# Sixteen partitions of a sample on each eighth partition, and the far zone of the caches copied in five-row packets, in a two-layer decoder trunk

## What is computed

```
h = rms_norm(x); a_val, a_glu, a_gate, b_val, b_gate, q, k, v, c_gate = split(h @ w_in)      # 1024 -> 3200
ya = silu(layer_norm(causal_conv31([state_conv, a_val * sigmoid(a_glu)]))) * silu(a_gate)
yb = pooled(b_val, windows 2/4/8/16) @ pool_w * scale * silu(b_gate)
q, k = rope(rms_norm(q)), rope(rms_norm(k))
kk, vv = [cache_k, k], [cache_v, v]
o = softmax attention over offsets 0..128, 0,4..512 and 0,16..2048 (three dilations, 129 keys each)
yc = o * silu(c_gate)
x = x + [ya, yb, yc] @ w_out
new_k, new_v = last 2048 rows of kk, vv        # per sample: the cache moved up by one row, and the new row
```

## Time and profile before

| what | us |
|---|---|
| median of three runs | 413.34 (411.63 to 413.67) |
| the profiled execution, on the device | 411.31 |
| its span, first to last instruction | 409.5 |
| PE, PEld busy | 347.4, 268.5 |
| DVE, ACT, POOL busy | 231.8, 99.2, 56.7 |
| moved by the DMA engines | 158.20 MB, mean 386 GB/s |

### The profile page before, as it was taken

One profiled execution on the slowest core, in us unless ns is written; L12 is line 12 of the kernel. 1 busy time (PEld: TensorE's weight loads), 2 busy tenths in 40 slices (PEclk: granted clock), 3 DMA queues, 4 the chain that ended last, 5 costly groups with the idle time before them and its releaser, 6 DMA issues.

```text
span 409.5 us, 4582 instructions
## 1 busy us (share of the span) xinstructions
PE 347.4 (85%) x1534; PEld 268.5 (66%) x1534; DVE 231.8 (57%) x518; ACT 99.2 (24%) x234; POOL 56.7 (14%) x100
## 2 busy tenths in 40 slices
PE   3899999977899699899799999974899699899500
PEld 2688888855677355788588888852677455688300
DVE  1526998898769734301326998898769654310100
ACT  3301144312533323011200135321623314001100
POOL 3702020202111112202022010202012022000000
PEclk9999999976899999999899999998899899999955
DMA  8999999999999999999999999999999999999993
GB/s 291 413 413 338 416 415 412 409 341 415 410 398 416 406 357 389 407 417 418 409 408 366 388 416 417 419 390 407 403 387 381 411 359 376 420 378 362 362 368 143
DMA packets 49033, 158.20 MB, mean 386 GB/s; under 512 B 5400, under 2 KB 19938, under 8 KB 47986
## 3 DMA queue, kind: packets, MB, share of 16 engines
q0 software_dynamic: 19968, 84.94, 53.4%
q1 hardware_dynamic: 19276, 38.16, 25.3%
q10 hardware_dynamic: 9766, 34.82, 21.5%
HBM read 139.35 MB, written 104.42 MB: 595 GB/s over the span
## 4 chain that ended last, share of the span: by engine, by line
PE 66%; DVE 20%; ACT 4%; issue 3%; DMA 1%; ACTq 0%; SPq 0%; DVEq 0%
PE pj L585 34%; PE pj L722 14%; PE psc L656 7%; DVE yc L1140 4%; DVE tok L1080 3%; DVE ssc L1083 3%; PE ptr L508 3%; DMA vt<-in_x_sample 1%; DVE spsum L1109 1%; PE ps L700 1%; PE psc L624 1%; PE ps L542 1%; PE psc L623 1%; ACT sc L882 1%; DVE sc L1045 1%
## 5 line engine op out<-in xcount | busy, mean ns | idle before, releaser
L585 PE MATMUL pj<-hT,wt 128*128 128x264 f32 x800 | 194.0, 401 | 3.4 <-DVE hT L995 3.4
L585 PEld LDWEIGHTS pj<-hT,wt 128*128 128x128 f32 x800 | 156.5, 199 | 34.8 <-issue 7.7
L1140 DVE SCALAR_TENSOR_TENSOR yc<-u_ext,cst,yc 128x256 f32<-128x256 f32 x180 | 76.2, 480 | 2.8 <-DVE u_smp L1023 0.6
L722 PE MATMUL pj<-mix,wt 128*128 128x264 f32 x256 | 59.5, 387 | 0.0
L722 PEld LDWEIGHTS pj<-mix,wt 128*128 128x128 f32 x256 | 48.0, 190 | 8.0
L503 POOL DMA_DIRECT2D out<-in_cache_v_win x48 | 28.2, 594 | 166.3 <-issue 166.3
L503 POOL DMA_DIRECT2D out<-in_cache_k_win x48 | 28.3, 596 | 136.9 <-issue 130.2
L1210 DVE TENSOR_TENSOR xT<-xT,pj 128x264 f32<-128x264 f32 x16 | 6.9, 430 | 53.2 <-PE pj L722 53.2
L656 PE MATMUL psc<-vt,spm 128*48 128x384 f32 x80 | 27.5, 495 | 0.0
L821 ACT ACTIVATE ex<-pj 128x264 f32<-128x264 f32 x22 | 8.6, 390 | 76.9 <-PE pj L585 62.7
L656 PEld LDWEIGHTS psc<-vt,spm 128*48 128x48 f32 x80 | 9.7, 126 | 14.9 <-issue 14.8
(11 more groups left out here) (165 smaller groups left out, 318.0 us busy)
## 6 DMA issues: line engine op xcount, KB each, us to landing
out<-in_cache_k_win POOLq DMA_DIRECT2D x32, 1080.0 KB, 76.7
out<-in_cache_v_win POOLq DMA_DIRECT2D x32, 1080.0 KB, 67.8
wt<-in_w ACTq DMA_DIRECT2D x21, 1536.0 KB, 16.2
out<-in_cache_k_win POOLq DMA_DIRECT2D x16, 432.0 KB, 71.6
out<-in_cache_v_win POOLq DMA_DIRECT2D x16, 432.0 KB, 65.2
kt<-in_cache_k_win SPq DMA_DIRECT2D x32, 144.0 KB, 27.6
vt<-in_cache_v_win SPq DMA_DIRECT2D x32, 144.0 KB, 24.6
kt<-in_cache_k_win SPq DMA_DIRECT2D x16, 192.0 KB, 14.8
```

Source lines behind the costliest of these rows:

```text
L585: last = nc.tensor.matmul(pj[n % RING][:, 0:T], w[:, k * P:(k + 1) * P], hT[:, k, :], start=(k == 0), stop=(k == KD - 1))
L722: last = nc.tensor.matmul(pj[n % RING][:, 0:T], w[:, k * P:(k + 1) * P], mix[:, k, :], start=(k == 0), stop=(k == KD - 1))
L1140: last = V.scalar_tensor_tensor(out=yc[:, t, 0:SEQ], in0=x_w, scalar=par[:, ROW_CW + w * CT + t:ROW_CW + w * CT + t + 1], in1=yc[:, t, 0:S ...
```

## The change

The code of layout: sample s now lies on partitions s, s + 8, ..., s + 120; gathers and write-backs run over the samples in their natural order; the first rows of the far zone and the new row of all samples are written by one transfer, not two. The constants (`sbias`, `mask`) and the copies to `rep` follow. The maximum over a sample's partitions goes through PE: `smaxT` turns the maxima, DVE reduces and spreads them, `smaxB` turns them back; `ssoft1` moves one projection later. And `PIECE_ROWS` is 5: a far run goes in three packets of 7680 B, a middle run in one of 4608 B as before.

```diff
-    20: [("probT", 3), ("score", 4), ("out", 2), ("ktok", 0), ("pnorm", 4), "ssoft1"],
-    21: [("probT", 4), ("score", 5), ("out", 3), ("ktok", 1), ("pnorm", 5)],
+    20: [("probT", 3), ("score", 4), "smaxT", ("out", 2), ("ktok", 0), ("pnorm", 4), "smaxB"],
+    21: [("probT", 4), ("score", 5), ("out", 3), ("ktok", 1), ("pnorm", 5), "ssoft1"],
-PIECE_ROWS = 3
+PIECE_ROWS = 5
-def sample_rows(s):
+def sample_rows(s, first=0):
 
-    first = 2 * PER_S * (s // 2) + s % 2
-    return slice(first, first + 2 * PER_S - 1, 2)
+    return slice(s + first * NS, P, NS)
...
-                for s in SAMPLE_ORDER:
+                for s in range(NS):
                     rows = one(f"cache_{kind}_win", l)[:, s, lo:lo + d * n * PER_S]
...
-                    sp.dma_start(rows, tile[r.start + 2 * skip:r.stop:2, at:at + n, :]).then_inc(S[name], 16)
+                    sp.dma_start(rows, tile[sample_rows(s, skip), at:at + n, :]).then_inc(S[name], 16)
                 if skip:
-                    for r in range(2):
-                        rows = out[:, r:NS:2, d - 1:d * n - 1]
-                        rows = rows.rearrange("o s (b e) h d -> (o s) b e (h d)", e=d)[:, :, 0, :]
-                        sp.dma_start(rows, tile[r:P:2 * PER_S, at + 1:at + n, :]).then_inc(S[name], 16)
+                    rows = out[:, :, d - 1:d * n - 1].rearrange("o s (b e) h d -> (o s) b e (h d)", e=d)[:, :, 0, :]
+                    sp.dma_start(rows, tile[0:NS, at + 1:at + n, :]).then_inc(S[name], 16)
...
+                    elif kind == "smaxT":
+
+                        pe.wait_ge(S["smax_ok"], nth(l, "smax_ok", 1))
+                        tr_use(step)
+                        turn(ptr[0:NH, 0:P], mx[:, :], P).then_inc(S["tr_full"], 1)
+                    elif kind == "smaxB":
+
+                        pe.wait_ge(S["smaxb_ok"], nth(l, "smaxb_ok", 1))
+                        tr_use(step)
+                        turn(ptr[:, 0:NH], mxb[:, :], NH).then_inc(S["tr_full"], 1)
...
-                        link(V.transpose(mx[:, 1, :], mx[:, 0, :]))
-                        link(V.tensor_reduce(mx2[:, :], mx[:, 1, :].rearrange("p (a g) -> p g a", g=2), AX.X, ALU.max))
-                        link(V.tensor_copy(mx[:, 2, :].rearrange("p (a g) -> p a g", g=2), mx2[:, None, :].to_broadcast([P, PER_S, 2])))
-                        link(V.transpose(mx[:, 3, :], mx[:, 2, :]))
-                        V.tensor_tensor(ssc[:, :, :], ssc[:, :, :], mx[:, 3, None, 0:NH].to_broadcast([P, SLOTS + 1, NH]),
-                                             ALU.subtract).then_inc(S["ssub"], 1)
...
+                    elif kind == "smaxT":
+
+                        dve.wait_ge(S["tr_full"], nth(l, "tr_full", TR[step] + 1))
+                        V.tensor_reduce(mx2[:, :], ptr[0:NH, 0:P].rearrange("h (a s) -> h s a", s=NS), AX.X, ALU.max).then_inc(S["tr_free"], 1)
...
+                    elif kind == "smaxB":
+
+                        dve.wait_ge(S["tr_full"], nth(l, "tr_full", TR[step] + 1))
+                        V.tensor_tensor(ssc[:, :, :], ssc[:, :, :], ptr[:, None, 0:NH].to_broadcast([P, SLOTS + 1, NH]),
+                                        ALU.subtract).then_inc(S["ssub"], 1)
```

More of the change, by code:

```diff
@@ L38 @@
 PER_S = P // NS
-PAIRS = NS // 2
-SAMPLE_ORDER = [s + PAIRS * e for s in range(PAIRS) for e in range(2)]
 SCALE = float(HD) ** -0.5
@@ L230, in constants @@
     bias = np.concatenate([log_of(multiplicity(i - j[:, :P])), log_of(multiplicity(P + i - j))], axis=1)
-    sample, a = 2 * (part // (2 * PER_S)) + part % 2, part[:, None] % (2 * PER_S) // 2
+    sample, a = part % NS, part[:, None] // NS
     offs = [PAST - (lo + d * (n * a + np.arange(n)[None, :])) for lo, d, n in GATHER]
@@ L300, in trunk_program @@
         so = rep[:, :, :].rearrange("p a b -> p (a b)")
-        mx = sb("mx", [P, 4, 32])
-        mx2 = sb("mx2", [P, 2])
+        mx = sb("mx", [P, NH])
+        mx2 = sb("mx2", [NH, NS])
+        mxb = sb("mxb", [NH, P])
         u_ext = sb("u_ext", [P, CT, TAIL + SEQ])
@@ L405, in put_back @@
                 skip = 1 if lo == 0 else 0
-                for s in SAMPLE_ORDER:
-                    r = sample_rows(s)
+                for s in range(NS):
                     rows = out[:, s, lo - 1 + d * n * skip:lo - 1 + d * n * PER_S]
                     rows = rows.rearrange("o (a b e) h d -> (o a) b e (h d)", b=n, e=d)[:, :, 0, :]
-                    sp.dma_start(rows, tile[r.start + 2 * skip:r.stop:2, at:at + n, :]).then_inc(S[name], 16)
+                    sp.dma_start(rows, tile[sample_rows(s, skip), at:at + n, :]).then_inc(S[name], 16)
                 if skip:
-                    for r in range(2):
-                        rows = out[:, r:NS:2, d - 1:d * n - 1]
-                        rows = rows.rearrange("o s (b e) h d -> (o s) b e (h d)", e=d)[:, :, 0, :]
-                        sp.dma_start(rows, tile[r:P:2 * PER_S, at + 1:at + n, :]).then_inc(S[name], 16)
+                    rows = out[:, :, d - 1:d * n - 1].rearrange("o s (b e) h d -> (o s) b e (h d)", e=d)[:, :, 0, :]
+                    sp.dma_start(rows, tile[0:NS, at + 1:at + n, :]).then_inc(S[name], 16)
             def states(l):
@@ L859, in _ @@
                         for t in range(AT):
-                            last = nc.scalar.copy(rep[:, t, :].rearrange("p (q a r) -> p q a r", q=PAIRS, r=2),
-                                                  src[:, t, SEQ:T].rearrange("p (q r) -> p q r", r=2)[:, :, None, :]
-                                                  .to_broadcast([P, PAIRS, PER_S, 2]))
+                            last = nc.scalar.copy(rep[:, t, :].rearrange("p (a s) -> p a s", s=NS),
+                                                  src[:, t, None, SEQ:T].to_broadcast([P, PER_S, NS]))
                         last.then_inc(S["rep_ok"], 1)
@@ L872, in _ @@
                         out = (o_k_s, o_v_s)[j]
-                        for r in range(2):
-                            act.dma_start(out[bass.ds(l, 1), r:NS:2, PAST - 1].rearrange("l s h d -> (l s) (h d)"),
-                                          kvb[r:P:2 * PER_S, j, :]).then_inc(S["new_out"], 16)
+                        act.dma_start(out[bass.ds(l, 1), :, PAST - 1].rearrange("l s h d -> (l s) (h d)"),
+                                      kvb[0:NS, j, :]).then_inc(S["new_out"], 16)
                     elif kind == "pnorm":
@@ L946, in _ @@
             V.memset(u_ext[:, :, 0:TAIL], 0.0)
-            V.memset(p_ext[:, :, 0:POOL_BUF], 0.0)
-            V.memset(mx[:, :, :], 0.0).then_inc(zeroed, 1)
+            V.memset(p_ext[:, :, 0:POOL_BUF], 0.0).then_inc(zeroed, 1)
             dve.wait_ge(zeroed, 1)
@@ L1216, in _ @@
             V.tensor_copy(y_tok[:, D_MODEL + 512:2 * D_MODEL], y_banks[1][1][:, :]).then_inc(y_half_copied, 1)
-DVE_LINKS = 40
+DVE_LINKS = 35
 _INS = ["x_prompt", "x_sample", "state_conv", "state_pool", "cache_k_win", "cache_v_win"]
```

16 lines of the change are left out of this document (11 added, 5 removed).

## The result

| | before | after |
|---|---|---|
| median | 412.49 (411.28 to 413.67, 4 runs) | 447.49 (445.18 to 448.38, 4 runs) |
| profiled execution, its span | 411.31, 409.5 | 448.38, 446.6 |

The ratio is 1.0837, 95% interval 1.0799 to 1.0875: the changed kernel takes 35 us longer. The forecast was 432 us and its range ended at 440. The direction was right and the size was not: 19 us forecast, 35 measured.

The account below looks back on a forecast made before the run. DMA transfers, drained at about 407 us, were taken to bound the kernel, arithmetic ending about 388. SP's last issue 387.84 + 38.3 = 426.1, output landing 428.1, span end 430.4, plus 1.8 outside: 432.2 us; range 413 to 440.

Parts of the forecast that it names:

- The bound and how it flips: Transfers drain at about 407 us, arithmetic ends at about 388; after the change, arithmetic waiting for late keys ends last.
- One packet per turn whatever its size: DMA queues alternate by single packets; a turn of the copies' queue q0 grows from 175.2 to 248.8 ns.
- fewer microseconds for q0 in all: Copies from cache to output need 6144 packets fewer at 9.8 ns each: 3.8 us less for each engine.
- wait of VectorE for keys in three parts: Sign: L1080 of layer 1 idle for some 35 us with a DMA named, in up to three waits.
- SP's wait for copies gone: Sign: SP's 19.4 us wait for copies at the end of the program disappears.
- low GB/s at the end: Sign: low transfer rate in the last slices, since q0 is done near 365 us.
- Weights: ACT's weight loads land 1.8 us later than their 16.2 us; hidden, with 5 us to spare.
- The rival of ports: Gathers collide in the new layout; the chain to the keys grows by up to 10 us: 436 to 443; chance 0.1.
- What that does to SP's queue: Layer 1's far keys: 694.5 packets per engine times 73.6 ns is 51.1 us, less 4.0; landing moves 47.1 to 317.3.
- Who waits: VectorE's fourth partial score of layer 1 waits 38.3 us; values possibly 2 us more, taken as 0.
- The softmax: Transposes move from VectorE to TensorE with two waits; taken as 0, bounds -1 and +3 us for both layers.
- The end: After SP's last issue at 426.1: output 2 us behind, 2.3 to the span's end, 1.8 outside the span.

Follow-up runs that it names:

- e1: The kernel before with PIECE_ROWS = 5 and nothing else of the change: 445.29 us, ratio 1.0786.
- e8: The changed kernel with PIECE_ROWS = 3 and smaxT and smaxB moved to where TensorE need not wait for VectorE: 416.38 us, ratio 1.0028.
- e10: The full change with smaxT moved behind pnorm 4 and smaxB behind score 5: 445.51 us, ratio 1.0692.
- e2: The changed kernel with PIECE_ROWS = 3, so new layout, single write-backs and softmax through TensorE alone: 413.93 us, ratio 1.0039.
- e5: The kernel before with PIECE_ROWS = 5 and without layer 0's write-back of the value rows: 402.17 us (one run; the kernel before 415.97).
- e9: The kernel before with PIECE_ROWS = 1, asking for copies in single rows: 414.98 us, ratio 0.9978.
- e4: The kernel before with pieces of 3 rows in the first 60 copies, 5 in the next 12, 15 in the last 24: 414.83 us, ratio 1.0029.
- e3: The kernel before with PIECE_ROWS = 15, one packet of 23040 B for a far run: 493.45 us, ratio 1.1935.

## Why the prediction was right and wrong

**Right.** The bound and how it flips: drain before, late keys after. One packet per turn whatever its size, 248.1 ns a turn (248.8 forecast), fewer microseconds for q0 in all, the wait of VectorE for keys in three parts, SP's wait for copies gone, low GB/s at the end (from 380 us on q0 moves nothing but one last packet; near 365 was forecast). Weights were hidden: the waits on them come to 0.7 us.

The Trainium skill (DMA: Bandwidth & Descriptors, section Queues, rings and completion order) has an engine drain a packet of 9 to 17 descriptors before it changes queue; the counts 665, 669, 670 here, with descriptors of 7680 B, do not show it. Even counts over 18 us would also come of bundles of even length, so shorter stretches have to decide: in the changed kernel, in the half microseconds from 60 to 62 us, q0, q1 and q10 moved 19, 17, 16; 16, 18, 18; 19, 19, 19; and 20, 19, 19 packets on 16 engines. That is about one of each for every engine each time, and in 36 such stretches from 56 to 74 us no queue moved fewer than 15 or more than 25. An engine that stayed with nine of q0's packets would be on them for over 2 us (9 x 248 ns), and such stretches would come out uneven. So the turns here go by single ones.

One reading of the prediction was loose: the 329 packets of q1 between 34 and 44 us average 2.6 KB, so most were not rows of 12 KB. Between 34 and 38 us they average 6.2 KB (87 packets, 0.54 MB), and q0 and q10 move 81 and 82 beside them, so what was read from it holds.

The rival of ports would have had the keys of the new layout later than those of e1; both came into use at 329.7. Partitions that share bits 2 to 4 and 6 share a port (the Trainium skill, SBUF — State Buffer, section Door 1: The DMA port swizzle). No run here shows a loss from that in the new layout.

**The step that failed first** is the sum under "What that does to SP's queue", where the landing moves "by 47.1". It moved by 329.6 - 270.2 = 59.4. Beside the earlier trace rows the same view of the kernel before has, from 25 to 270.3 us:

```profile
q10 hardware_dynamic: 7086, 25.88, 26.7%
```

Each engine's time in the stretch, by the queues' shares, splits the difference. q0: 0.520 x 245.3 = 127.6 before, 0.588 x 304.6 = 179.1 after, so 51.5 and not 47.1. The turns that q0 had to itself did fall away, nearly as reckoned: it moved 738.4 packets per engine before and 719.6 after, 18.8 fewer, 3.2 us (22.6 and 4.0 reckoned). But the longer turn is paid on all 719.6, also on those that q0 still takes beside q1, and I had charged it to q1's 694.5 alone; and in this stretch a turn grew from 172.8 to 248.9 ns, by 76.1 and not 73.6. That is 54.8 us in place of 51.1. q1: 58.6 to 60.3, 1.7. q10: 0.267 x 245.3 = 65.5 before, 71.3 after, so 5.8, the largest part that was missing. In a stretch 59 us longer ACT's queue moved 637 packets more. I had held the packets of the others fixed while the window grew. With three queues in turn, what the third has ready in the longer window has to be counted too. Together 59.0 us. This split is worked out from the shares; no run took q10's packets out to test its part.

**The second** is "Who waits" with "The softmax" and their zeros. "q10 has no load while the arithmetic stands, so I take 0" has a premise that nearly holds: in the changed kernel q10 moved nothing from 290 to 297 us, and from 297 to 329.6, while VectorE waited for key rows, 279 packets beside q1's 1349. The 0 did not follow from it: in e1 the values land at 380.3, TensorE waits 3.19 us for them and then runs its 16 multiplications in 7.03 us (5.9 before, from 325.83 to 331.71; the prediction took 326.47 for its start, 0.6 us late). The 2 us that I set aside as possible were due, and the product starts 50.6 us behind the far keys' first use, not 46.8. In the changed kernel the slower softmax hides this wait and costs more: 54.1 - 46.8 = 7.3 us between the far keys and the values' product. Of these 3.1 are the one projection at 6.83 us, 2.3 are waits ahead of it (0.43, 1.08 and 0.74), which the kernel before did not have. Most of the rest lies just ahead of the product: a wait of 4.19 us for the convolution where there were two of 1.56, and six multiplications behind it in 3.01 us, at a granted clock of 0.50, where they took 2.05. The bound I gave to the softmax was 3 us for both layers. It priced waits, and not TensorE's clock behind them. e8 shows that order of steps to be the cause in layer 0, where the projection goes back to 3.80 us; in the full change it is not shown apart (e10).

**The end** was over-reckoned by 3.5 us. SP's last issue took 0.34 us, not 2.02 (1.7; e2, in which copies still run at that time, has 0.35, so it isn't the copies, and the cause is open). And 4.25 us lie between the last issue and the end, where 6.1 were counted (1.8).

The sum: 432.2 + 12.3 (keys) + 7.3 (softmax, clock, values) - 3.5 = 448.3; the profiled execution took 448.38.

The range failed with the same two terms: its upper end took either ports or values, both as small things, and held no case in which the forecast mechanism itself was larger.

## What to carry to other kernels

Where queues share the DMA engines packet by packet, as here, the length of a background queue's packets sets the pace of the others. Count the packets of the transfer that somebody waits for, multiply by the sum of one turn of each queue, and ask when it is needed. Take packets out of the queue that is waited for: 2040 fewer were worth 43 to 46 us here once the queue was late (e5). Shortening the packets of what nobody waits for would be the other way, and is not shown here: the single rows of e9 did not reach the queue. Long packets late in the run are not free either: the write-backs in the queues beside them can come to set the end (e4). When you stretch such a window, let every queue bring what it has ready for the longer time, and carry on to the next transfer behind it.

## What the hardware showed that I had not expected

- TensorE's granted clock fell to 0.50 in a stretch of small operations, behind a wait of 1.08 us (busy for 5.49 of the 7 us up to then): the projection of 16 multiplications next to come took 6.64 us against 3.73, busy throughout. With a single wait of 0.72 us there it took 3.80.
- Single-row pieces of 1536 B left the queue with the same 19968 packets as three-row pieces, and only POOL's time went up, from 56.7 to 72.1 us.
- 6144 packets fewer by cutting to 7680 B saved about 4 us of each engine, but 3840 fewer (e4) saved 0.7 and 12288 fewer (e3) 1.2, both mostly by packets of 23040 B.
